# Sample-state updates of a hybrid decoder step: matmuls moved into the routing, sums kept in memory and added to the states at the end

## The chip, the cores and the metric

The kernel runs on one core of one Trainium2 chip. The metric is the device time of one execution, in microseconds (us). A core has five engines that run side by side and meet in semaphores: PE (TensorE, matmuls), DVE (VectorE), ACT (ScalarE), POOL (GpSimd) and SP (SyncE, which here only issues transfers). 16 DMA engines move data between memory and the on-chip SBUF; matmuls write to eight PSUM banks of 128 x 512 floats.

## The reference

One inference step of a one-layer decoder trunk, for 512 prompt tokens and 8 sample sequences of 4 tokens (T = 544 rows of width 1024). A token mixer is followed by a mixture of 16 experts:

```
proj = x @ w_in                                   # q, f, v, g and three conv parts
S_new = exp(b_last) * S + einsum('bhsk,bhkv->...', k * exp(b_last - b), v)   # state, per head
o     = rms(q-part of the state and of the chunk) * silu(g)
x1    = layer_norm(ALPHA * x + concat[o, yc] @ w_out)
probs = softmax(x1 @ w_router + bias); best group of 4, then its best 2 experts
y     = sum_e gate_e * (silu(x1 @ w_gate[e]) * (x1 @ w_up[e])) @ w_down[e]
out   = layer_norm(ALPHA * x1 + y)
```

For the samples the old state (8 sequences x 4 heads x 128 x 128, 2 MB) is an input and the new one an output: per sequence and head, new = decay * old + k^T v over the sequence's four tokens. This sum k^T v, the sample update, is what the change is about.

## The kernel before

All matmuls that matter for accuracy split each float32 operand into a rounded high part and a low part and run three products (ACT makes the high part, DVE the low one by a subtraction of two SBUF operands). The work runs in stages, each engine with its own program order:

- **Input projection and recurrence** (to about 266 us). POOL forms exponents (`exponents`, L575), DVE decays q and k (`decayed`, L1017), PE the pairs.
- **Output projection** (266 to 322 us and on). PE runs `mix(half, conv, tt)` (L1627): 12 matmuls for each of five token tiles, for two halves of the columns and two halves of the rows of w_out. DVE adds each tile to the residual (`add_mix`, L1152) and normalises. Behind `mix(0, False, tt)`, tt below 4, PE makes head tt's sample updates (`sample_updates`, L1639): two fp32 matmuls of 32 rows, 128 keys by 512 value columns, four sequences each. So that a matmul forms the sums of single sequences, POOL first copies the head's values into `v_msk`, once per sequence and zero elsewhere (`mask_values`, L613). There is one `v_msk` buffer, so head h waits for head h-1's matmuls. DVE forms the new states from banks 1 and 2 and the old states `s0` (`new_states`, L1164), eight operations a head. When all are made, SP stores `s0` (L480), loads ln2's parameters (L482), waits for the store (L510) and only then loads the first expert weights, since `raw[3]` and `raw[4]` lie where `s0` lay.
- **Router and routing** (322 to 375 us). PE transposes x1 and makes the logits (`turn_x1`, `logits`). DVE then runs one chain of some 60 small operations (L1211 to L1286): softmax, group and expert choice, rank (after PE's matmuls L1719, L1721), slots, and the table of token ids (after PE's L1731). In its waits PE runs `keep_clock(n)`, idle matmuls without a reader: 16 before the rank, 12 before the slots and 28 behind them. POOL gathers the rows of the first two experts' tokens from memory (`gather`, L625); PE transposes them (`x_turn`), ACT and DVE split them.
- **Experts** (375 to 666 us). Sixteen steps in a fixed order, each with six weight chunks of 1 MB, loaded by SP into a ring of eight raw buffers, split by ACT (`mhi`) and DVE (`mlo`), and used by PE. POOL stores each expert's rows to memory and gathers the next expert's tokens. `xg` holds two blocks of gathered rows.
- **End** (666 to 705 us). POOL waits for the last row store and gathers each token's two expert rows; PE weighs and sums them with diagonal matrices (`weigh`, L1837), DVE, ACT and POOL normalise, SP stores (L556, L558).

There is a branch for tokens beyond an expert's first 128; here no step of it runs, and nothing of it shows in the trace.

Of the kernel before, what the change touches and what calls it, by code (L numbers as in the profile page):

```python
# [42 lines left out]
H = 4  # L43
# [72 lines left out]
def build(nc, a):  # L116
# [5 lines left out]
    with ctx:  # L122

        x1_dram = nc.dram_tensor("x1_by_token", (T, D), F32, kind="Internal").ap()
        yg_dram = nc.dram_tensor("y_by_slot", (NBLK * P, D), F32, kind="Internal").ap()
# [29 lines left out]
        raw += [fa(68 * K, 2048), fa(68 * K + 2 * H * T, 2048)]  # L155
        s0 = fa(32 * K, 4096).rearrange("p (b h v) -> p b h v", b=DB, h=H)
        A0 = 48 * K
        xn = fa(A0, NTT * D).rearrange("p (t n) -> p t n", t=NTT)
# [23 lines left out]
        k_tok_s = fa(Q0 + H * T, 512).rearrange("p (h k) -> p h k", h=H)  # L182
        v_msk = fa(Q0 + H * T + 512, DB * P).rearrange("p (b v) -> p b v", b=DB)
        h_gain = fa(Q0 + H * T + 1536, 512)
# [21 lines left out]
        wr = fa(Z0, KT * E).rearrange("p (k e) -> p k e", k=KT)  # L206
        silu_g, hbuf = fa(64 * K, 512), fa(66 * K, 512)
        ysb = [fa(U0, D), fa(U0 + D, D)]
        diag = fa(Z0, (1 + 2 * NTT) * P).rearrange("p (i r) -> p i r", i=1 + 2 * NTT)
# [26 lines left out]
        s_su, s_st, s_o, s_oc = sem("state_update"), sem("state_ready"), sem("o_made"), sem("o_copied")  # L236
        s_vm, s_sus, s_s0n, s_sto = sem("v_masked"), sem("sample_update"), sem("sample_state"), sem("sample_states_stored")
        s_stp = sem("prompt_state_stored")
        s_selt, s_sel = sem("groups_transposed"), sem("groups_t_ready")
# [70 lines left out]
        def x_place(m):  # L310

            n = P if m % NTT < 4 else NS
            c0 = P if m == 2 * NTT - 1 else 0
            return bank[x_bank(m)][:, c0:c0 + 4 * n]

        def sum_banks(tt):
# [108 lines left out]
        def _(sp):  # L425
# [52 lines left out]
            sp.dma_start(rt[:, 448:464], a["router_bias"].unsqueeze(0).broadcast_to([P, E])).then_inc(s_wr, 16)  # L478
            sp.wait_ge(s_s0n, 2 * H)
            sp.dma_start(a["out_hgrn_sample"][0].rearrange("b h k v -> k b h v"), s0).then_inc(s_sto, 16)  # L480
            for i, name in ((2, "ln2_g"), (3, "ln2_b")):
                sp.dma_start(ln[:, i, :], a[name].broadcast_to([P, D])).then_inc(s_lnp2, 16)  # L482

# [25 lines left out]

            sp.wait_ge(s_sto, 16)  # L510
            load(3, source(5, 0, None))
# [10 lines left out]
            for tt in range(NTT):  # L522
                sp.wait_ge(s_x1, tt + 1)
                rows = P if tt < 4 else NS
                sp.dma_start(x1_dram[tt * P:tt * P + rows, :], xr[0:rows, tt, :]).then_inc(s_x1s, 16)
            load(6, source(2, 1, 0))
            moe_loads(1, 1, (4, 5))
            moe_loads(2, 2, (0,))
# [7 lines left out]
            moe_loads(E, E, (2, 3))  # L536

            sp.wait_ge(s_slot, 3)
            n_over = sp.value_load(itab[0:1, 0:1], min_val=0, max_val=NOV)
            with sp.If(0 < n_over):  # L540
                with sp.Fori(0, NOV // RING) as i:
                    for r in range(RING):
                        v = RING * i + r
                        with sp.If(v < n_over):
                            e = sp.value_load(itab[0:1, bass.ds(v + 1, 1)], min_val=0, max_val=E - 1)
                            for o, j in enumerate(OV_ORDER):
                                sp.wait_ge(m_lo, 6 * E + 6 * v + o + 1 - NRAW)
                                load(6 * E + 6 * r + o, source(j, e, e))

            for tt in range(NTT):  # L550
# [15 lines left out]
        def _(pool):  # L566
# [46 lines left out]
            def mask_values(h):  # L613
                nc.gpsimd.tensor_tensor(v_msk[0:NS], v_tok[0:NS, 4, h * P:(h + 1) * P].unsqueeze(1).broadcast_to([NS, DB, P]),
                                        seq_mask, ALU.mult).then_inc(s_vm, 1)
# [4 lines left out]
            nc.gpsimd.memset(xr[:, 4, :], 0.0).then_inc(s_xr0, 1)  # L620
            for h in range(1, H):
                pool.wait_ge(s_sus, 2 * h)
                mask_values(h)
# [8 lines left out]
            pool.wait_ge(s_x1s, 16 * NTT)  # L632
            pool.wait_ge(s_ids, 1)
            gather(0, 0)
            gather(1, 1)
            pool.wait_ge(m_t, 1)
# [23 lines left out]
            n_over = pool.value_load(itab[0:1, 0:1], min_val=0, max_val=NOV)  # L660
            with pool.If(0 < n_over):  # L661
                for v in range(NOV):
# [19 lines left out]
        def _(act):  # L682
# [158 lines left out]

            for n, j in enumerate((0, 1, 4)):
                act.wait_ge(m_raw[n], 16)
                nc.scalar.activation(split[split_slot(0, j)][0], raw[n], ACT.Copy).then_inc(m_hi, 1)


# [20 lines left out]
            def silu(bi):  # L867
                act.wait_ge(m_use, gate_count(bi))
                if not (isinstance(bi, int) and bi == 0):
                    act.wait_ge(m_h, bi)  # L870
                nc.scalar.activation(silu_g, bank[2][:, :], ACT.Silu).then_inc(m_sg, 1)
# [76 lines left out]
        def _(dve):  # L948
# [214 lines left out]

            def new_states(h):  # L1164

                for g in range(2):
                    dve.wait_ge(s_sus, 2 * h + g + 1)
                    for i in range(4):
                        bi = 4 * g + i
                        last = stt(s0[:, bi, h, :], s0[:, bi, h, :], s0_decay[:, bi * H + h:bi * H + h + 1],  # L1170
                                   bank[1 + g][:, i * P:(i + 1) * P], ALU.mult, ALU.add)
                    last.then_inc(s_s0n, 1)

            dve.wait_ge(s_o, NTT)
# [203 lines left out]
            with dve.If(0 < n_over):  # L1378
                with dve.Fori(0, NOV // RING) as i:
                    for r in range(RING):  # L1380
                        v, par = RING * i + r, r % 2
                        with dve.If(v < n_over):
# [12 lines left out]
                            dve.wait_ge(m_st[par], 16 * (E // 2 + r // 2) + 8 * RING * i)  # L1395
                            nc.vector.tensor_copy(ysb[par][:, 512:D], bank[6][:, :]).then_inc(m_yd, 1)

            ts_(diag[:, 0, :], ident, ALPHA, None, ALU.mult).then_inc(s_diag, 1)
            for tt in range(NTT):
                rows = P if tt < 4 else NS  # L1400
                for n in range(2):
                    ts_(diag[0:rows, 1 + 2 * tt + n, 0:rows], ident[0:rows, 0:rows],
                        gw[0:rows, n * NTT + tt:n * NTT + tt + 1], None, ALU.mult).then_inc(s_diag, 1)
            dve.wait_ge(s_lnp2, 32)

# [23 lines left out]
        def _(pe):  # L1429
# [264 lines left out]
            for n in range(6):  # L1694
                last_mix(n)
            pe.wait_ge(s_s0n, 2 * H)
            pe.wait_ge(s_wc, NTT)
# [12 lines left out]

            def keep_clock(n):

                idle = RA[:, 32 * K + KT * T:32 * K + KT * T + 640]
                for _ in range(n):
                    mm(bank[0][:, :], idle[:, 512:640], idle[:, 0:512], start=True, stop=True)

            keep_clock(16)
            pe.wait_ge(s_oh, 1)
# [5 lines left out]

            keep_clock(12)
            for n in range(2):
# [74 lines left out]

            keep_clock(28)
            x_turn(0, 0)
# [80 lines left out]
```

## Time and profile before

| | us |
|---|---|
| median of 3 runs | 703.26 (702.64 to 706.01) |
| the profiled execution: its own time | 706.77 |
| its span, first to last instruction | 704.9 |
| PE, DVE, ACT, POOL busy | 671.2, 503.6, 344.3, 134.9 |
| mean granted TensorE clock | 0.974 of full speed |
| moved by DMA | 162.56 MB |

The profile is of one execution. A row of a timeline has the start in us from the span's begin, the duration in us, engine, line, operation, tiles out<-in, shapes and how many instructions are merged (x12), and in brackets how long the engine had been idle and who released it. One fp32 matmul stands as two records. The granted clock is 1.00 for 2.4 GHz and 0.50 for 1.2 GHz.

### The profile page before, as it was taken

What the parts mean: (1) busy time and instruction counts of PE and PEld (TensorE: products, weight loads), DVE (VectorE), ACT (ScalarE), POOL (GpSimd) and SP (SyncE); (2) the same over time, 40 slices, a digit from 0 to 9 for tenths busy, and PEclk for the clock granted to TensorE, in tenths of its full rate; (3) what the DMA queues carried; (4) which work ended last, traced back from release to release, by engine and by line L of the source; (5) the groups of instructions that cost most, each with busy time, mean ns of one, the idle gap of its engine ahead of it and who ended that gap; (6) DMA issues with size and microseconds to landing.
All of it is one profiled execution on the core that took longest, in us unless ns stands there. A gap on an engine that the chain in (4) does not pass through costs nothing. (4 is left out here: it accounts for less than half of the span.)

```text
span 704.9 us, 9687 instructions
## 1 busy us (share of the span) xinstructions
PE 671.2 (95%) x3863; PEld 563.5 (80%) x3863; DVE 503.6 (71%) x576; ACT 344.3 (49%) x338; POOL 134.9 (19%) x81
## 2 busy tenths in 40 slices
PE   6999999988999999999978999999999999999796
PEld 5999899988997887567856888888888888888531
DVE  4326346799666284757495999999999999999526
ACT  4438412222236231011415777777777777777302
POOL 0000414433031210400021011111111111100064
PEclk9999999999999999999799999999999999999997
DMA  9951111211613005069227999999999999993163
GB/s 288 382 185 61 60 60 61 70 53 58 202 43 109 23 16 191 0 209 419 97 84 304 364 377 416 410 402 419 413 402 415 404 410 410 411 405 148 60 248 133
DMA packets 48689, 162.56 MB, mean 231 GB/s; under 512 B 4294, under 2 KB 23450, under 8 KB 36364
## 3 DMA queue, kind: packets, MB, share of 16 engines
q1 hardware_dynamic: 41756, 136.62, 51.0%
q0 software_dynamic: 6896, 25.43, 9.2%
q8 instruction: 25, 0.41, 0.2%
q14 instruction: 12, 0.10, 0.0%
HBM read 142.61 MB, written 19.44 MB: 230 GB/s over the span
## 5 line engine op out<-in xcount | busy, mean ns | idle before, releaser
L1309 DVE TENSOR_TENSOR RA<-FA,RA 128x2048 fp32r<-128x2048 f32 x93 | 212.8, 2289 | 28.6 <-ACT RA L854 28.0
L854 ACT ACTIVATE RA<-FA 128x2048 fp32r<-128x2048 f32 x93 | 178.9, 1924 | 45.0 <-PE bank L1753 28.9
L1753 PE MATMUL bank<-RA 128*128 128x512 f32 x768 | 186.1, 398 | 2.3 <-DVE RA L1314 2.1
L1753 PEld LDWEIGHTS bank<-RA 128*128 128x128 f32 x768 | 142.3, 190 | 34.0 <-DVE RA L1314 3.0
L1491 PE MATMUL bank<-RA 128*128 128x272 f32 x432 | 110.4, 292 | 0.0
L1492 PE MATMUL bank<-RA 128*128 128x272 f32 x432 | 109.7, 290 | 0.0
L1765 PE MATMUL bank<-RA 128*128 128x512 f32 x384 | 89.9, 390 | 1.4 <-DVE RA L1319 1.4
L1765 PEld LDWEIGHTS bank<-RA 128*128 128x128 f32 x384 | 72.0, 188 | 16.5 <-DVE RA L1319 1.6
L1491 PEld LDWEIGHTS bank<-RA 128*128 128x128 f32 x432 | 82.6, 191 | 0.0
L1492 PEld LDWEIGHTS bank<-RA 128*128 128x128 f32 x432 | 82.4, 191 | 0.0
L978 DVE TENSOR_TENSOR RA<-FA,RA 128x2048 fp32r<-128x2048 f32 (+1 forms) x18 | 48.6, 2700 | 28.6 <-ACT RA L712 28.3
L712 ACT ACTIVATE RA<-FA 128x2048 fp32r<-128x2048 f32 (+1 forms) x18 | 33.6, 1866 | 59.9 <-PE bank L1635 30.9
L1484 PE MATMUL bank<-RA 128*128 128x256 f32 (+1 forms) x480 | 58.8, 282 | 2.0 <-ACT FA L724 2.0
L1484 PEld LDWEIGHTS bank<-RA 128*128 128x128 f32 (+1 forms) x480 | 56.2, 172 | 4.6 <-ACT FA L724 2.4
L1635 PE MATMUL bank<-RA 128*128 128x512 f32 (+1 forms) x240 | 59.4, 405 | 0.0
L628 POOL DMA_INDIRECT FA<-x_by_token,ids x16 | 39.8, 2485 | 83.5 <-DVE ids L1286 65.1
L1635 PEld LDWEIGHTS bank<-RA 128*128 128x128 f32 (+1 forms) x240 | 41.7, 177 | 17.0 <-issue 3.2
L645 POOL DMA_DIRECT2D y_by_slot<-FA x16 | 9.1, 571 | 236.6 <-DVE FA L1326 236.6
L583 POOL TENSOR_TENSOR FA<-FA 128x1024 f32<-128x1024 f32 (+1 forms) x7 | 16.6, 2368 | 112.9 <-PE bank L1526 67.8
L759 ACT ACTIVATE FA<-FA 128x2048 f32<-128x2048 f32 (+1 forms) x7 | 13.6, 1946 | 49.6 <-POOL FA L584 49.6
L1037 DVE COPY_PREDICATED FA<-masks,bank 128x512 f32<-128x512 uint8 x28 | 20.1, 734 | 22.2 <-PE bank L1526 21.7
L1526 PE MATMUL bank<-FA 128*128 128x128 f32 x256 | 30.9, 278 | 3.9 <-DVE FA L1037 3.9
(227 smaller groups left out, 764.9 us busy)
## 6 DMA issues: line engine op xcount, KB each, us to landing
FA<-w_up SPq DMA_DIRECT2D x32, 1024.0 KB, 7.3
FA<-w_gate SPq DMA_DIRECT2D x32, 1024.0 KB, 6.9
FA<-w_down SPq DMA_DIRECT2D x32, 1024.0 KB, 7.7
FA<-w_in SPq DMA_DIRECT2D x13, 1024.0 KB, 5.0
y_by_slot<-FA POOLq DMA_DIRECT2D x16, 512.0 KB, 7.7
y_by_slot<-FA POOLq DMA_DIRECT2D x1, 4096.0 KB, 17.1
FA<-w_out SPq DMA_DIRECT2D x4, 1024.0 KB, 5.1
FA<-x_prompt SPq DMA_DIRECT2D x8, 256.0 KB, 5.8
```

Source lines behind the costliest of these rows:

```text
L628: pool.indirect_dma_start(out=xg[par], out_offset=None, in_=x1_dram, in_offset=bass.IndirectOffsetOnAxis(ap=ids[:, bi:bi + 1].bitcast(U32) ...
L712: nc.scalar.activation(split[o % 2][0][:, cs], raw[o % 3][:, cs], ACT.Copy).then_inc(s_hi, 1)
L854: nc.scalar.activation(split[split_slot(bi, j)][0], raw[place], ACT.Copy).then_inc(m_hi, 1)
L978: tt_(split[o % 2][1][:, cs], raw[o % 3][:, cs], f(split[o % 2][0][:, cs]), ALU.subtract).then_inc(s_lo, 1)
L1309: tt_(sl[1], raw[place], f(sl[0]), ALU.subtract).then_inc(m_lo, 1)
L1484: last = mm(pb[0:rows, 0:CW], xT[x_][:, kt, tok(j)], w_[:, kt, :], start=(kt == 0 and i == 0), stop=(kt == KT - 1 and i == 2))
L1491: mm(pb[:, 0:HT], lhs, xT[x_][:, kt, 0:HT], start=first, stop=end)
L1492: last = mm(ps[:, 0:HT], lhs, xT[x_][:, kt, HT:T], start=first, stop=end)
L1526: last = mm(bank[4 + p % 3][:, cols], lf[:, h, cols], rf[:, h, cols], start=True, stop=True)
L1635: last = mm(w_bank(half, tt)[0:rows, :], xT[x_][:, k0 + kt, tok(tt)], w_[:, kt, :], start=(conv and kt == 0 and i == 0), stop=(not conv an ...
L1753: last = mm(out[:, :], xgT[par][x_][:, kt, :], w[w_][:, t, :], start=(kt == 0 and i == 0), stop=(kt == KT - 1 and i == 2))
L1765: last = mm(bank[5 + g][:, :], hT[x_][:, kt, :], w[w_][:, t, 512 * g:512 * g + 512], start=(kt == 0 and i == 0), stop=(kt == 3 and i == 2))
```

## The change

The sample updates leave the output projection. PE makes heads 0 and 1 behind the logits in place of 12 of the 16 idle matmuls, head 2 behind the rank in place of 12, and head 3 behind the slots with 16 idle ones instead of 28. ACT copies each of the eight results from its bank into SBUF (`su_out`), between the first expert's weight copies. SP stores each head's 512 KB to memory (`su_dram`) ahead of the loads of expert 1's up weights; ln2's parameters are loaded behind the last expert's weights. POOL has two buffers for the masked values, and its second gather waits until all four stores have landed (its target shares space with `su_out[3]`). SP no longer stores states or waits ahead of the first expert loads. When the last weights are split, SP loads the old states again (2 MB) and the four updates (4 x 512 KB); DVE adds them with 32 operations behind the gate diagonals, and SP stores the new states ahead of the outputs.

```diff
@@ memory and SBUF
+        su_dram = nc.dram_tensor("sample_updates", (H, P, DB * P), F32, kind="Internal").ap()
+        s0_end = fa(48 * K, 4096).rearrange("p (b h v) -> p b h v", b=DB, h=H)
-        v_msk = fa(Q0 + H * T + 512, DB * P).rearrange("p (b v) -> p b v", b=DB)
+        v_msk = [fa(off, DB * P).rearrange("p (b v) -> p b v", b=DB)
+                 for off in (Q0 + H * T + 512, AT0 + NTT * D - 2 * H * T)]
+        su_out = [fa(off, DB * P) for off in (U0, U0 + DB * P, 64 * K, 60 * K)]
+        su_end = [fa(off, DB * P).rearrange("p (b v) -> p b v", b=DB) for off in (Q0, Q0 + DB * P, B0, B0 + DB * P)]
+        def update_bank(n):
+            return bank[(0, 1, 2, 3, 7, 0, 1, 2)[n]]
@@ SP
-            sp.wait_ge(s_s0n, 2 * H)
-            sp.dma_start(a["out_hgrn_sample"][0].rearrange("b h k v -> k b h v"), s0).then_inc(s_sto, 16)
-            for i, name in ((2, "ln2_g"), (3, "ln2_b")):
-                sp.dma_start(ln[:, i, :], a[name].broadcast_to([P, D])).then_inc(s_lnp2, 16)
...
-            sp.wait_ge(s_sto, 16)
             load(3, source(5, 0, None))
...
             load(6, source(2, 1, 0))
+            for h in range(H):
+                sp.wait_ge(s_sue, 2 * h + 2)
+                sp.dma_start(su_dram[h], su_out[h]).then_inc(s_sud, 16)
             moe_loads(1, 1, (4, 5))
...
             moe_loads(E, E, (2, 3))
+            sp.wait_ge(s_sud, 16 * H)
+            for i, name in ((2, "ln2_g"), (3, "ln2_b")):
+                sp.dma_start(ln[:, i, :], a[name].broadcast_to([P, D])).then_inc(s_lnp2, 16)
+            sp.wait_ge(m_lo, 6 * E - 2)
+            sp.wait_ge(m_t, E)
+            states_again()
+            sp.wait_ge(m_lo, 6 * E - 1)
+            updates_again(0)
+            updates_again(1)
+            sp.wait_ge(m_lo, 6 * E)
+            updates_again(2)
+            updates_again(3)
...
+            sp.wait_ge(s_s0n, H)
+            sp.dma_start(a["out_hgrn_sample"][0].rearrange("b h k v -> k b h v"), s0_end).then_inc(s_sto, 16)
             for tt in range(NTT):
@@ POOL
             mask_values(0)
             pool.wait_ge(s_stp, 16)
             pool.wait_ge(s_o, NTT)
             nc.gpsimd.memset(xr[:, 4, :], 0.0).then_inc(s_xr0, 1)
-            for h in range(1, H):
-                pool.wait_ge(s_sus, 2 * h)
+            mask_values(1)
+            for h in range(2, H):
+                pool.wait_ge(s_sus, 2 * (h - 1))
                 mask_values(h)
...
             pool.wait_ge(s_ids, 1)
+            pool.wait_ge(s_vm, H)
             gather(0, 0)
+            pool.wait_ge(s_sud, 16 * H)
             gather(1, 1)
@@ ACT
-            for n, j in enumerate((0, 1, 4)):
+            def copy_update(n):
+                act.wait_ge(s_sus, n + 1)
+                nc.scalar.activation(su_out[n // 2][:, 512 * (n % 2):512 * (n % 2) + 512], update_bank(n)[:, :],
+                                     ACT.Copy).then_inc(s_sue, 1)
+
+            def first_hi(n, j):
                 act.wait_ge(m_raw[n], 16)
                 nc.scalar.activation(split[split_slot(0, j)][0], raw[n], ACT.Copy).then_inc(m_hi, 1)
+            for n in range(4):
+                copy_update(n)
+            first_hi(0, 0)
+            first_hi(1, 1)
+            for n in range(4, 2 * H):
+                copy_update(n)
+            first_hi(2, 4)
@@ DVE
-            def new_states(h):
...
-                if tt < H:
-                    new_states(tt)
...
+            dve.wait_ge(s_end, 16 * (H + 1))
+            for h in range(H):
+                for bi in range(DB):
+                    last = stt(s0_end[:, bi, h, :], s0_end[:, bi, h, :], s0_decay[:, bi * H + h:bi * H + h + 1],
+                               su_end[h][:, bi, :], ALU.mult, ALU.add)
+                last.then_inc(s_s0n, 1)
             dve.wait_ge(s_lnp2, 32)
@@ PE
                 for g in range(2):
-                    if h:
-                        pe.wait_ge(s_s0n, 2 * h + g - 1)
-                    mm(bank[1 + g][:, :], k_tok_s[0:NS, h, :], v_msk[0:NS, 4 * g:4 * g + 4, :],
+                    n = 2 * h + g
+                    if n >= 5:
+                        pe.wait_ge(s_sue, n - 4)
+                    mm(update_bank(n)[:, :], k_tok_s[0:NS, h, :], v_msk[h % 2][0:NS, 4 * g:4 * g + 4, :],
                        start=True, stop=True).then_inc(s_sus, 1)
...
                 mix(0, False, tt)
-                if tt < H:
-                    sample_updates(tt)
...
-            keep_clock(16)
+            sample_updates(0)
+            sample_updates(1)
+            keep_clock(4, bank[5])
             pe.wait_ge(s_oh, 1)
...
-            keep_clock(12)
+            sample_updates(2)
...
-            keep_clock(28)
+            sample_updates(3)
+            pe.wait_ge(s_sue, 4)
+            keep_clock(16, bank[3])
             x_turn(0, 0)
```

## Rows read from the trace of the kernel before

**Rows 1.** The page's first part: busy us, share of the span, instructions

```profile
PE 671.2 (95%) x3863; PEld 563.5 (80%) x3863; DVE 503.6 (71%) x576; ACT 344.3 (49%) x338; POOL 134.9 (19%) x81
```

**Rows 2.** Timeline of PE, 290 to 297 us: head 2's sample updates

```profile
294.37 1.98 PE L1645 MATMUL bank<-FA 32*128 32x512 f32 x4 [0.54 <-POOL FA L614]
296.28 1.24 PE L1635 MATMUL bank<-RA 128*128 128x512 f32 x3
```

**Rows 3.** Timeline of PE, 346 to 385 us: routing and first expert

```profile
348.26 5.39 PE L1715 MATMUL bank<-RA 128*128 128x512 f32 x16
355.15 0.22 PE L1719 MATMUL bank<-FA 128*128 128x96 bf16 x1 [1.50 <-DVE FA L1247]
...
360.66 0.50 PE L1731 MATMUL bank<-FA 128*128 128x24 bf16 x10 [2.32 <-DVE FA L1283]
...
371.26 1.23 PE L1743 MATMUL bank<-FA 128*128 128x128 f32 x8 [1.05 <-DMA FA<-x_by_token,ids]
374.63 7.35 PE L1753 MATMUL bank<-RA 128*128 128x512 f32 x24 [2.14 <-DVE RA L1314]
381.82 1.12 PE L1743 MATMUL bank<-FA 128*128 128x128 f32 x8
```

**Rows 4.** Busy time by stretch: PE, PEld, DVE, ACT, POOL, clock, DMA, GB/s

```profile
348.00:351.00 3.00, 3.00 (x14) 2.39 (x13) 2.09 (x12) 1.76 (x2) 0.00 (x0) 0.50 0.00 0
```

**Rows 5.** Timeline of DVE, 341 to 375 us: ends of the routing chain

```profile
348.37 0.23 DVE L1211 TENSOR_TENSOR FA<-bank,FA 128x64 f32<-128x64 f32 x1 [7.00 <-PE bank L1670]
...
362.51 6.69 DVE L1301 TENSOR_TENSOR RA<-FA,RA 128x2048 fp32r<-128x2048 f32 x3
...
373.29 1.29 DVE L1314 TENSOR_TENSOR RA<-bank,RA 128x512 fp32r<-128x512 f32 x2
```

**Rows 6.** Timeline of ACT, 280 to 388 us: the first three weight copies

```profile
349.42 5.50 ACT L844 ACTIVATE RA<-FA 128x2048 fp32r<-128x2048 f32 x3
```

**Rows 7.** Timeline of POOL: an exponent subtraction and head 1's mask

```profile
105.41 3.94 POOL L584 TENSOR_TENSOR FA<-FA 128x1024 f32<-128x1024 f32 x1
...
286.00 1.89 POOL L614 TENSOR_TENSOR FA<-FA 32x1024 f32<-32x1024 f32 x1 [18.96 <-PE bank L1645]
```

**Rows 8.** Timeline of DVE: beside those, and the other steps used

```profile
107.52 2.98 DVE L1024 TENSOR_TENSOR FA<-FA 128x1088 f32<-128x1088 f32 x1
110.42 1.28 DVE L1025 TENSOR_TENSOR FA<-FA 128x1088 f32<-128x1088 f32 x1
...
268.10 0.69 DVE L1136 TENSOR_TENSOR FA<-FA 128x512 f32<-128x512 f32 x1
...
285.38 2.14 DVE L1170 SCALAR_TENSOR_TENSOR FA<-FA,bank 128x128 f32<-128x128 f32 x8
```

**Rows 9.** Transfers by line: KB each, median us from issue to landing

```profile
y_by_slot<-FA POOLq DMA_DIRECT2D x16, 512.0 KB, 7.7
...
out_hgrn_sample<-FA SPq DMA_DIRECT2D x1, 2048.0 KB, 9.3
...
FA<-x_by_token,ids POOLq DMA_INDIRECT x16, 10.9
FA<-y_by_slot,slot_i POOLq DMA_INDIRECT x10, 6.3
...
FA<-state_hgrn SPq DMA_DIRECT2D x1, 0.5 KB, 12.2
```

**Rows 10.** The chain that ended last: start us, us, what

```profile
673.82 0.98 POOL FA L671
...
675.10 6.20 DMA FA<-y_by_slot,slot_i
...
681.34 16.72 PE bank L1841 x36
```

**Rows 11.** Timeline of DVE, 655 to 685 us: last weight split, end

```profile
659.64 2.28 DVE L1309 TENSOR_TENSOR RA<-FA,RA 128x2048 fp32r<-128x2048 f32 x1
...
681.19 1.30 DVE L1412 BATCH_NORM_STATS2 FA<-bank 128x6 f32<-128x512 f32 x2 [11.98 <-PE bank L1841]
```

More of the change, by code:

```diff
@@ L237, in build @@
         s_vm, s_sus, s_s0n, s_sto = sem("v_masked"), sem("sample_update"), sem("sample_state"), sem("sample_states_stored")
+        s_sue, s_sud, s_end, s_ovd = (sem("sample_update_copied"), sem("sample_update_stored"), sem("states_and_updates_in"),
+                                      sem("overflow_done"))
         s_stp = sem("prompt_state_stored")
@@ L536, in _, with states_again, updates_again @@
             moe_loads(E, E, (2, 3))
+            def states_again():
+                sp.dma_start(s0_end, a["state_hgrn"][0].rearrange("b h k v -> k b h v")).then_inc(s_end, 16)
+            def updates_again(h):
+                sp.dma_start(su_end[h].rearrange("p b v -> p (b v)"), su_dram[h]).then_inc(s_end, 16)
+            sp.wait_ge(s_sud, 16 * H)
[10 more added lines that the diff above has]
+            updates_again(3)
             sp.wait_ge(s_slot, 3)
@@ L540, in _ @@
             with sp.If(0 < n_over):
+                sp.wait_ge(s_end, 16 * (H + 1))
                 with sp.Fori(0, NOV // RING) as i:
@@ L548, in _ @@
                                 load(6 * E + 6 * r + o, source(j, e, e))
+                sp.wait_ge(s_ovd, 1)
+                states_again()
+                for h in range(H):
+                    updates_again(h)
+            sp.wait_ge(s_s0n, H)
+            sp.dma_start(a["out_hgrn_sample"][0].rearrange("b h k v -> k b h v"), s0_end).then_inc(s_sto, 16)
             for tt in range(NTT):
@@ L613, in mask_values @@
             def mask_values(h):
-                nc.gpsimd.tensor_tensor(v_msk[0:NS], v_tok[0:NS, 4, h * P:(h + 1) * P].unsqueeze(1).broadcast_to([NS, DB, P]),
+                nc.gpsimd.tensor_tensor(v_msk[h % 2][0:NS], v_tok[0:NS, 4, h * P:(h + 1) * P].unsqueeze(1).broadcast_to([NS, DB, P]),
                                         seq_mask, ALU.mult).then_inc(s_vm, 1)
@@ L661, in _ @@
             with pool.If(0 < n_over):
+                pool.wait_ge(s_end, 16 * (H + 1))
                 for v in range(NOV):
@@ L868, in silu @@
                 act.wait_ge(m_use, gate_count(bi))
-                if not (isinstance(bi, int) and bi == 0):
+                if isinstance(bi, int) and bi == 0:
+                    act.wait_ge(s_sud, 16 * H)
+                else:
                     act.wait_ge(m_h, bi)
@@ L1162, in add_mix @@
                 chain[0] += 1
-            def new_states(h):
[L1166 to L1172, printed above, removed]
             dve.wait_ge(s_o, NTT)
@@ L1396, in _ @@
                             nc.vector.tensor_copy(ysb[par][:, 512:D], bank[6][:, :]).then_inc(m_yd, 1)
+                nc.vector.memset(rt[:, 441:442], 0.0).then_inc(s_ovd, 1)
+                dve.wait_ge(s_end, 32 * (H + 1))
             ts_(diag[:, 0, :], ident, ALPHA, None, ALU.mult).then_inc(s_diag, 1)
@@ L1403, in _ @@
                         gw[0:rows, n * NTT + tt:n * NTT + tt + 1], None, ALU.mult).then_inc(s_diag, 1)
+            dve.wait_ge(s_end, 16 * (H + 1))
+            for h in range(H):
+                for bi in range(DB):
+                    last = stt(s0_end[:, bi, h, :], s0_end[:, bi, h, :], s0_decay[:, bi * H + h:bi * H + h + 1],
+                               su_end[h][:, bi, :], ALU.mult, ALU.add)
+                last.then_inc(s_s0n, 1)
             dve.wait_ge(s_lnp2, 32)
@@ L1695, in _ @@
                 last_mix(n)
-            pe.wait_ge(s_s0n, 2 * H)
             pe.wait_ge(s_wc, NTT)
@@ L1709, in _, with keep_clock @@
             logits(NTT - 1).then_inc(s_lg, 1)
-            def keep_clock(n):
+            def keep_clock(n, to):
                 idle = RA[:, 32 * K + KT * T:32 * K + KT * T + 640]
                 for _ in range(n):
-                    mm(bank[0][:, :], idle[:, 512:640], idle[:, 0:512], start=True, stop=True)
-            keep_clock(16)
+                    mm(to[:, :], idle[:, 512:640], idle[:, 0:512], start=True, stop=True)
+            sample_updates(0)
+            sample_updates(1)
+            keep_clock(4, bank[5])
             pe.wait_ge(s_oh, 1)
@@ L1800, in step @@
                 gate_up(bank[3], par, split_slot(bi, 5), 1, count_of(bi, 5))
-            keep_clock(28)
+            sample_updates(3)
+            pe.wait_ge(s_sue, 4)
+            keep_clock(16, bank[3])
+            pe.wait_ge(s_sue, 2 * H)
             x_turn(0, 0)
```

## The prediction

> **What bounds the kernel now.** The page comes first: PE is busy for 95% of the span [rows 1], so each stage is asked whether PE waits there. In the output projection (266 to 348 us) it is the bound: its timeline has no gap but one of 0.54 us, ahead of head 2's state updates [rows 2]. One head's updates (four records: two fp32 matmuls of two passes) hold PE from 294.37 to 296.28, 1.91 us [rows 2], and there are four heads. In the routing (348 to 375 us) it is not: DVE starts at 348.37 when the logits end and runs one serial chain to 362.5 [rows 5]; PE fills its waits with idle matmuls and still sits idle 1.50, 2.32 and 1.05 us, then 2.14 us for DVE's low half of the gathered x [rows 3]. At the end the chain is the row gather that lands at 681.3 and then 16.7 us of PE [rows 10].
>
> **The change, part by part.**
> 1. *Updates out of the projection.* PE loses 4 x 1.91 = 7.6 us and the 0.54 us stall, 8.2 us. DVE loses four groups of eight state operations at 2.14 us [rows 8], which lay in its waits: nothing. Late next would be the second half's low weights, but they hang on the end of the first half's last matmul, which moves along. So the logits end 8.2 us sooner: **-8.2**. Bounds: -7.6 (the stall reappears) to -8.2.
>
> 2. *The second mask moves.* POOL forms head 1's masked values now right behind its memset at about 267.1 us, 1.89 us long [rows 7], two SBUF inputs. Does that touch DVE? At 105.41 a POOL tensor_tensor ran to 109.35 [rows 7]; DVE's multiply, started at 107.52, took 2.98 us, while the same kind took 1.28 right behind [rows 8]. It ended 1.2 us after POOL did: it had waited for all of it. DVE operations with one input in PSUM are not held: eight of them took their usual 2.14 us beside the mask of 286.00 [rows 7, 8]. At 268.10 DVE scales head outputs, two SBUF inputs, 0.69 us [rows 8]; it would be held to 269.0, and the transposition on PE that waits for it comes with it: **+0.85** (0 to 1.2, if PE cannot hide it).
>
> 3. *Updates 0 and 1 in the wait for the choice.* The 16 idle matmuls took 5.39 us at a clock that began at half (0.50 [rows 4], the 1.2 GHz level, after the 16-column logits). Eight update records cost about 3.2 us at the half clock (3.3 of them) and 4.7 x 0.48 = 2.2 us at full, and four idle ones at most 1.0 (half an update record each or less): 6.4 us, against the 6.9 from 348.26 to 355.15 [rows 3]. Nothing on PE itself; 0 to +2.5 if the clock stayed low (twice 3.8 and twice 0.9 make 9.4 us).
>
> 4. *Masks 2 and 3 in the routing.* This is the term that I count highest. They are released when updates 0 and 1 are done (about 352 and 354 us in the old times), and run 1.89 us each while DVE is in its chain of small operations, most of which read two SBUF operands, each waiting for the one before. By rows 7 and 8 the first such operation waits for the end of the mask. A reduction or two with one input may pass, so 1.7 us each: **+3.4**. PE then idles some 4 us ahead of the rank matmuls, and the clock falls: **+0.2** for six short matmuls. Bounds 0 (no hold on such small operations) and 2 x 1.89 + 0.3 = +4.1.
>
> 5. *ACT.* Eight copies of a bank join, about 0.6 us each by estimate (512 columns, where a weight copy of 2048 takes 5.50/3 = 1.8 us [rows 6]). Six and two of the three weight copies fit into ACT's old gap. The third weight copy stands behind copies 6 and 7, and these behind head 3's update, which is issued behind the slot matmuls. In old times: these end at about 362.3, just ahead of DVE's 362.51 [rows 5]; update to 364.2 at full clock or 366.1 at half; copy 7 to 364.8 or 366.7; the weight copy 1.8 us more, so 366.6 or 368.5. DVE wants it 2 x 2.2 us after 362.51, at 366.9 [rows 5]. Late by 0 or 1.6 us; DVE's next steps run without a gap to 373.29 [rows 5] and release PE at 374.63 [rows 3]. **+0.9**, bounds 0 and 1.9.
>
> 6. *Stores of the updates and the second gather.* Four stores of 512 KB pass through SP ahead of expert 1's up weights, which are needed a step later: nothing. POOL's second gather now waits for the last store. That is issued about 367 (old times) and lands in 3 to 7.7 us (the store of a y block [rows 9]); a gather takes 10.9 [rows 9]: 381 to 386. PE wants it at 381.82 [rows 3], which steps 4 and 5 move by 4.5 to 386.3. I take 0, bounds 0 and +3. The first six expert loads start up to 40 us sooner, behind nothing that they can delay: 0.
>
> 7. *The tail.* The update reads follow the last weight split, which ends at 661.9 [rows 11]; with 7.7 us they are in by 669.6. The 2 MB of old states, 12.2 us [rows 9], are asked for some 9 us earlier. The last y store shares their last microsecond: **+0.4** (0 to 1.5). DVE then has 32 state operations, at 2.14/8 us each 8.6 us, and 11.98 us of idle time ahead of 681.19 to put them in [rows 8, 11]: begun by 669.6 they end by 678.2. Nothing, with 3 us in hand. They now read two SBUF operands, so each row gather on POOL waits for the one under way: **+0.4**. The store of the new states, 2 MB in 9.3 us when little else ran [rows 9], starts at about 678, among the gathers that feed PE (6.3 us each [rows 9]). The gather issued at 675.10 (tile 1's first) lands at 681.3, and the next follow at 1.28 us [rows 10], so tile 2's land at about 683.9 and 685.1; PE, at 16.72/9 = 1.86 us for each, takes them at 685.1 and 686.9: 1 to 2 us in hand. A gather in the expert loop takes 10.9 us beside weight loads instead of 6.3, so sharing is felt. I take **+1.0**, from 0 up to the case in which the two queues share the DMA engines evenly: what lands at 683.9 then lands 6 us after that, and PE is 5 to 5.7 us late.
>
> Here a page matters. The Trainium skill, "DMA: Bandwidth & Descriptors", section "Queues, rings and completion order", says that a DMA engine takes turns between queues by whole packets of typically 9 to 17 descriptors. By that a turn of the 512-byte rows of the state store would be as long as a turn of the gather or longer, and the tail would cost 5.7 instead of 1.0. No row of the kernel before shows a store of short rows beside a gather; I read it as one row per turn, which favours the gather's 4 KB rows.
>
> **Sum.** -8.2 + 0.85 + 3.6 + 0.9 + 0.4 + 0.4 + 1.0 = -1.05 us. The profiled execution took 706.8 us (span 704.9), the median of the runs is 703.26; taken off the median that is **702.2 us**. A measurement of this kernel can tell about 0.5%, 3.5 us, from no change.
>
> **The rivals.**
> - *The masks hold DVE little* (chance 0.22). The routing's operations take 0.15 to 0.3 us, and no row shows POOL beside such short ones. Against it: nothing in rows 7 and 8 depends on length. Terms 2 and 4 fall away: -1.05 - 4.45 = -5.5 us, 697.8.
> - *The state store starves the last gathers* (0.13, with the masks holding DVE). Place: the gathers of tiles 2 and 3, from 678 us. Price 5.7 in place of 1.0: +3.65 us, 706.9. It makes the change slower than before as soon as it costs over 2 us. For it: the 10.9 us of the expert loop. Against: PE, not the gathers, sets the pace from 681.3 on [rows 10].
> - *The second gather comes late* (0.07). If the last update store and the gather, with the weight loads behind them, take 2 us more each than their rows 9, the gather lands at 390 against 386.3: +3.7 to the sum, +2.65, 705.9.
> - *The change doesn't do what it says* (0.05). If the projection were held by something else that ended at the same time, the updates would leave 2 us of gain only: +5, 708.4. PE's gapless timeline speaks against it.
> - *As forecast* (0.53): 702.2, own range 699.5 to 705.
>
> **How the numbers follow.** Within 0.5% is 699.7 to 706.8. Of the forecast's 0.53 I put 0.06 below, 0.44 within, 0.03 above. The first rival gives 0.18 below and 0.04 within; the two late-gather rivals, whose centres lie near the upper edge, 0.09 within and 0.11 above; the fifth case 0.05 above. So faster 0.24, the same 0.57, slower 0.19. The range reaches from the first rival's centre to a little past the starved tail: 697.7 to 708.0.
>
> **What would show it.** The projection ends and the logits end some 7.3 us sooner (341, not 348.3). In the routing, two DVE operations with two SBUF inputs last about 1.9 us instead of 0.24, each ending with a POOL mask, and the first expert's first matmul stands at 374.6 - 7.3 + 4.5 = 371.8 us. The third weight split of expert 0 waits for ACT by 0 to 1.6 us. PE's second transposition waits for no DMA. In the tail DVE's 32 operations end by 678, and PE waits under 1.5 us more for gathers than now. I am wrong if DVE's chain of 14 us keeps its length (then the first rival), or if PE has gaps between tiles at the end (then the second), or if the logits end at 343 or later.

## The result, and the profile after

The changed kernel takes 711.94 us (median of 4 executions, 709.45 to 712.88) against 704.63 (702.64 to 706.71) for the kernel before in the same sitting: ratio 1.0108, 95% interval 1.0078 to 1.0138. It is 7.3 us slower, where 1 us faster was forecast, and lies outside the forecast range.

The profiled execution of after is the fastest of its four (709.45, span 707.6), that of before one of its slower ones (706.77, span 704.9). So the two traces differ by only 2.7 us. They show where time came and went; how much it is in all, the medians say.

| stretch, us | before | after | difference | forecast |
|---|---|---|---|---|
| mixing stage, from its 272.6 / 272.2 to its end | 49.6 | 39.0 | -10.6 | -8.2 |
| logits' end to expert 0's first matmul | 26.4 | 31.2 | +4.8 | +4.5 |
| expert 0's first matmul to the last y store's issue | 292.2 | 292.2 | 0.0 | 0 |
| last y store's issue to the end | 38.1 | 48.8 | +10.7 | +1.8 |

In these two traces the last y store is issued 8.0 us sooner, at 658.82 instead of 666.80, and the end gave back 10.7. The 8.0 hold 2.2 us that the table does not show: 0.4 ahead of the mixing stage, and 1.8 between its end and the logits' end. That last part is 26.0 us long in before and 24.3 in after, and 23.8 to 26.2 in the eleven other traces of the changed kernel and its variants, by where in it the granted clock falls to 0.50; its 1.8 us are chance. So is the 0.0 in the third row: in the repeat of the change that stretch takes 294.6 us.

The first part of the page of after, and then the busy time by stretch, of before and of after (columns as in [rows 4]):

```profile
PE 665.0 (94%) x3827; PEld 555.9 (79%) x3827; DVE 507.5 (72%) x576; ACT 349.7 (49%) x346; POOL 138.0 (20%) x81
```

```profile
296.20:300.80 4.60, 4.60 (x13) 3.35 (x12) 1.82 (x8) 0.00 (x0) 1.89 (x1) 0.63 0.01 4
```

```profile
296.20:300.80 4.60, 4.60 (x22) 3.71 (x21) 2.29 (x1) 0.50 (x1) 0.00 (x0) 1.00 0.23 28
...
336.00:339.00 3.00, 3.00 (x4) 1.00 (x3) 2.35 (x14) 0.87 (x2) 0.00 (x0) 0.50 0.00 0
354.00:357.00 3.00, 3.00 (x5) 0.89 (x4) 3.00 (x2) 1.14 (x3) 2.15 (x1) 0.50 0.04 10
360.00:363.00 3.00, 2.78 (x17) 2.28 (x15) 2.69 (x11) 0.18 (x1) 0.95 (x1) 1.00 0.97 373
666.00:668.00 2.00, 2.00 (x6) 0.71 (x4) 2.00 (x9) 0.00 (x0) 2.00 (x1) 1.00 0.00 0
...
680.00:682.00 2.00, 2.00 (x4) 0.97 (x3) 0.00 (x0) 0.00 (x0) 1.60 (x2) 0.50 1.04 410
```

PE's busy share fell from 95% [rows 1] to 94%: work left PE, but idle time came. Before, the matmuls behind head 2's updates ran at a mean granted clock of 0.63 (13 in 4.6 us); after, 22 stand in the same window at 1.00. In the routing the clock is 0.50 from the logits to behind 357 us, updates and all. From 666 to 668, where the row gathers should go out, DVE and POOL are both busy all the time and no DMA engine moves a byte.

The routing, PE's timeline of after (answers to [rows 3]):

```profile
335.46 7.19 PE L1694 MATMUL bank<-FA 32*128 32x512 f32 x8
342.58 2.08 PE L1761 MATMUL bank<-RA 128*128 128x512 f32 x4
345.22 0.26 PE L1767 MATMUL bank<-FA 128*128 128x96 bf16 x1 [0.56 <-DVE FA L1287]
...
352.67 3.76 PE L1694 MATMUL bank<-FA 32*128 32x512 f32 x4
356.35 5.48 PE L1761 MATMUL bank<-RA 128*128 128x512 f32 x16
361.67 1.12 PE L1791 MATMUL bank<-FA 128*128 128x128 f32 x8
366.62 7.28 PE L1801 MATMUL bank<-RA 128*128 128x512 f32 x24 [3.84 <-DVE RA L1354]
373.74 1.12 PE L1791 MATMUL bank<-FA 128*128 128x128 f32 x8
```

The timelines of DVE and of POOL, after, in the same stretch (answer to [rows 5, 7]):

```profile
339.23 0.24 DVE L1269 TENSOR_TENSOR FA<-FA 128x80 f32<-128x80 f32 x1
339.50 1.82 DVE L1270 TENSOR_TENSOR FA<-FA 128x80 f32<-128x80 f32 x1
...
343.01 0.24 DVE L1271 TENSOR_REDUCE FA<-FA 128x5 f32<-128x80 f32 x1
343.28 1.55 DVE L1272 TENSOR_TENSOR FA<-FA 128x80 f32<-128x80 f32 x1
...
358.89 2.29 DVE L1341 TENSOR_TENSOR RA<-FA,RA 128x2048 fp32r<-128x2048 f32 x1 [1.45 <-ACT RA L886]
```

```profile
339.32 1.90 POOL L647 TENSOR_TENSOR FA<-FA 32x1024 f32<-32x1024 f32 x1 [71.45 <-PE bank L1694]
342.74 1.99 POOL L647 TENSOR_TENSOR FA<-FA 32x1024 f32<-32x1024 f32 x1 [1.51 <-PE bank L1694]
```

Two operations of 0.24 us last 1.82 and 1.55, and each ends some 0.1 us behind a mask (341.22, 344.73): +2.9 us. A reduction with one input, at 343.01, runs beside the second mask in its usual 0.24. The first four updates (eight records) take 7.19 us and the four idle matmuls 2.08, 9.3 together. The third weight split waits 1.45 us for ACT. Nothing stands ahead of PE's second transposition at 373.74: the second gather is in time.

The end of after: DVE's and POOL's timelines, the queue of SP, and PE.

```profile
662.62 8.49 DVE L1449 SCALAR_TENSOR_TENSOR FA<-FA 128x128 f32<-128x128 f32 x32 [1.40 <-DMA FA<-sample_updates]
```

```profile
658.82 0.53 POOL L681 DMA_DIRECT2D y_by_slot<-FA  x1 [9.36 <-DVE FA L1366]
665.61 6.36 POOL L708 DMA_INDIRECT FA<-y_by_slot,slot_i  x1 [6.26 <-issue]
672.28 0.98 POOL L708 DMA_INDIRECT FA<-y_by_slot,slot_i  x1 [0.31 <-issue]
```

```profile
659.43 8.83 PE L1892 MATMUL bank<-FA 128*128 128x512 f32 x16 [1.88 <-DVE FA L1440]
678.99 21.72 PE L1892 MATMUL bank<-FA 128*128 128x512 f32 x44 [10.73 <-DMA FA<-y_by_slot,slot_i]
```

The transfers of after (answers to [rows 9]):

```profile
sample_updates<-FA SPq DMA_DIRECT2D x4, 512.0 KB, 2.6
FA<-sample_updates SPq DMA_DIRECT2D x4, 512.0 KB, 7.8
out_hgrn_sample<-FA SPq DMA_DIRECT2D x1, 2048.0 KB, 21.4
...
FA<-y_by_slot,slot_i POOLq DMA_INDIRECT x10, 10.2
```

The chain of after (answers to [rows 10]):

```profile
665.61 13.25 DMA FA<-y_by_slot,slot_i
...
678.99 21.73 PE bank L1892 x44
```

The first row gather occupies POOL for 6.36 us instead of 0.98: it ends 0.9 us behind the last of the 32 additions (662.62 + 8.49 = 671.11). That is +5.4 us. The store of the new states starts when the additions end, together with this gather, and PE, which waits for it, starts 7.0 us after its end at 671.97. In before the first gather, issued at 672.53 and as long as the next one, 0.98 us, was over at 673.51, and PE began 3.5 us later. PE's timeline of before:

```profile
676.98 1.95 PE L1841 MATMUL bank<-FA 128*128 128x512 f32 x4 [0.74 <-DMA FA<-y_by_slot,slot_i]
```

That is +3.6 us. From there to PE's last matmul before took 21.1 us and after takes 21.7: +0.7. After its long pause PE begins at the half clock (0.50 at 680 to 682), while before it ran at 1.00 with short waits for gathers. And the first gather starts 6.8 us behind the y store's issue instead of 5.7: +1.1. Together 10.7 (rounded parts). No experiment isolates the +1.1. It is also there without the additions (6.5 us), and it is gone (5.1 to 5.3) in the three traces of the change and its variants in which the y store goes out some 1.5 us later against the reads of the updates. That fits the prediction's term for the y store sharing time with these reads, forecast at 0.4.

### The profile page after: what moved, and what is told of

The parts are those of the page before. It is cut to its first block and busy times, and to the rows that moved or that the text cites. A ratio compares the mean times of both kernels' runs of the same rounds, so it can differ in the third digit from the quotient of the medians.

```text
span 707.6 us, 9633 instructions
## 1 busy us (share of the span) xinstructions
PE 665.0 (94%) x3827; PEld 555.9 (79%) x3827; DVE 507.5 (72%) x576; ACT 349.7 (49%) x346; POOL 138.0 (20%) x81
## 5 line engine op out<-in xcount | busy, mean ns | idle before, releaser
L1683 PE MATMUL bank<-RA 128*128 128x512 f32 (+1 forms) x240 | 56.8, 395 | 0.0
L662 POOL DMA_INDIRECT FA<-x_by_token,ids x16 | 38.9, 2433 | 29.9 <-PE bank L1791 12.2
L1892 PE MATMUL bank<-FA 128*128 128x512 f32 (+1 forms) x60 | 30.5, 671 | 12.6 <-DMA FA<-y_by_slot,slot_i 10.7
```

What stands on the lines that cost most here:

```text
L662: pool.indirect_dma_start(out=xg[par], out_offset=None, in_=x1_dram, in_offset=bass.IndirectOffsetOnAxis(ap=ids[:, bi:bi + 1].bitcast(U32) ...
L1683: last = mm(w_bank(half, tt)[0:rows, :], xT[x_][:, k0 + kt, tok(tt)], w_[:, kt, :], start=(conv and kt == 0 and i == 0), stop=(not conv an ...
L1892: ins = mm(bank[i][0:rows, :], diag[0:rows, d, 0:rows], src[0:rows, tt, 512 * g:512 * g + 512], start=first, stop=last)
```

## The experiments

Each ran beside the kernel before, in one of three sittings; its medians there were 704.17, 703.63 and 704.23 us. A ratio is worked out from all executions of its own sitting, and is not quite that of the two medians.

**The end: moving the store, and taking the additions out.** First, SP waits for the last gathers before it stores the states; second, the same without the additions:

```diff
             sp.wait_ge(s_s0n, H)
+            for n in range(2):
+                sp.wait_ge(s_ga[NTT - 1][n], 16)
             sp.dma_start(a["out_hgrn_sample"]...
```

```diff
-            for h in range(H):
-                for bi in range(DB):
-                    last = stt(s0_end[:, bi, h, :], ...)
-                last.then_inc(s_s0n, 1)
+            nc.vector.memset(rt[:, 441:442], 0.0).then_inc(s_s0n, H)
```

> The change with one edit: SP issues the store of the new states only when the last two row gathers have landed. Theory A (the 32 state additions, two SBUF inputs each and back to back, hold POOL's first row gather until the last of them) expects the first gather on POOL still about 6.4 us long, but landing 3.3 us after it, as before the change, instead of 6.9: the first sum on PE 3 to 4 us sooner than in the change, time 3 to 4 us below the change. Rival B (the state store in the DMA queues is the whole loss) expects the long first gather gone too and the time 8 us or more below the change. Rival C (the loads of states and updates delay the last y store) expects no more than 1 us.

> The run e2 without the 32 state additions (they are left out; a memset gives their signal). Theory A expects POOL's first row gather back at 1.0 us and the time 5 to 6 us below e2, some 8 us below the kernel before, with the front of the change kept whole. Rival B expects no difference to e2. Rival C (transfers, not the additions) expects the gap from the last y store to the first gather's end to stay at 13 us.

Measured: 708.61 us, ratio 1.0075 (1.0042 to 1.0107), and 700.70 us, 0.9952 (0.9927 to 0.9977). The timeline of POOL with the store last, and without the additions:

```profile
667.94 6.36 POOL L710 DMA_INDIRECT FA<-y_by_slot,slot_i  x1 [6.18 <-issue]
674.61 0.98 POOL L710 DMA_INDIRECT FA<-y_by_slot,slot_i  x1 [0.30 <-issue]
```

```profile
668.04 0.98 POOL L710 DMA_INDIRECT FA<-y_by_slot,slot_i  x1 [5.93 <-issue]
669.32 0.98 POOL L710 DMA_INDIRECT FA<-y_by_slot,slot_i  x1 [0.30 <-issue]
```

With the store out of the way the gather is held as long as ever. Without the additions it is not held, and 7.9 us are gone, more than the 5 to 6 expected. Yet that kernel, whose output lacks the additions, is only 3.4 us below before, where some 8 were expected: the front is worth less by the medians than by the two traces, whose 8.0 us hold 2.2 of chance. The store's own part is the first of these against the change: PE waits 7.06 us instead of 10.73, 3.7 less in the traces; by the ratios (1.0075 against 1.0086 and 1.0108) 1 to 2 us, which the intervals can't tell from nothing.

**The additions in pieces.** They stay, and DVE waits for its own completion behind every second one (with the store last, and with the store where the change has it); then the change with one such wait behind each head's eight, three of which stand between additions:

```diff
                 for bi in range(DB):
                     last = stt(s0_end[:, bi, h, :], ...)
+                    if bi % 2 and bi < DB - 1:
+                        link(last)
                 last.then_inc(s_s0n, 1)
+                dve.wait_ge(s_s0n, h + 1)
```

```diff
                 last.then_inc(s_s0n, 1)
+                dve.wait_ge(s_s0n, h + 1)
```

> The run e2 with DVE waiting for its own completion behind every second state addition. If POOL gets the shared port only when DVE's queue runs dry for a moment (theory A1), the first gather takes 1 to 2 us and the time is 3 to 5 us below e2, though the additions take longer. If any running sequence of such additions keeps POOL out regardless of short breaks (A2), the first gather lasts until the last addition, 6.4 us or more, and the time is that of e2 or 1 to 3 us above.

> The change with the breaks between the additions, the state store left where the change has it. The run with both edits was 0.35% under the kernel before. If the hold of the first gather is the main loss and the store a smaller one, this run's gathers start in time, the state store starts at about 674 beside the fourth gather, and the last gathers are 2 to 4 us late: 702 to 705 us. If PE, not the gathers, sets the pace there (as the prediction had it), the store costs under 1 us: 700 to 702.

> The change with only three breaks in the additions: DVE waits for its own completion behind each head's eight. If POOL gets the port only where DVE's queue runs dry (A1), the first gather ends behind the first break after its start, so it lasts 1 to 3.3 us instead of 6.4, and the next gathers wait likewise, about 2.3 us apart, until the additions end at the same place as before: time 3 to 6 us below the change, above the run with 15 breaks. If the length of each single addition matters rather than the breaks, the first gather stays at 6 us.

Measured: 700.53 us, 0.9965 (0.9934 to 0.9996); 700.61, 0.9954 (0.9927 to 0.9981); 700.27, 0.9951 (0.9926 to 0.9977). The change itself in the same sitting as the second:

> The change itself, unedited, on the chip of the next three runs: 7 to 8 us above the kernel before (709 to 712 us), POOL's first row gather 6.4 us long and landing 13 us after its start, the clock of the updates in the routing at the half level as in the first profile (0.50 from 336 to 357 us).

It took 710.35 us, 1.0086 (1.0045 to 1.0127), its first gather 6.54 us. The timelines of the third kernel (a wait behind each eight), DVE's and POOL's, and its transfers:

```profile
663.43 8.87 DVE L1449 SCALAR_TENSOR_TENSOR FA<-FA 128x128 f32<-128x128 f32 x32
```

```profile
666.41 0.98 POOL L708 DMA_INDIRECT FA<-y_by_slot,slot_i  x1 [4.81 <-issue]
667.70 1.00 POOL L708 DMA_INDIRECT FA<-y_by_slot,slot_i  x1 [0.30 <-issue]
669.00 1.09 POOL L708 DMA_INDIRECT FA<-y_by_slot,slot_i  x1 [0.30 <-issue]
```

```profile
out_hgrn_sample<-FA SPq DMA_DIRECT2D x1, 2048.0 KB, 17.1
FA<-y_by_slot,slot_i POOLq DMA_INDIRECT x10, 8.1
```

Three waits that cost DVE 0.4 us (8.87 against 8.49) bring the ratio from 1.0086 to 0.9951, 9.5 us, and turn the loss into a gain of 4. They are worth as much as the removal of the additions: nothing else of the additions costs time that these runs can tell. Against the expectations, the first gained 8.1 us where 3 to 5 were expected, the third 9.5 where 3 to 6 were, and the second is where it was put if PE sets the pace (700 to 702). With the waits in, the place of the store matters no more (0.9965 and 0.9954), though the gathers' median landing is 8.1 us beside it. My expectation that a gather would wait up to the next break was wrong. The groups end at about 665.6, 667.9 and 670.1 (an estimate: four equal parts of the 8.87 us), and the gather of 666.41 began and ended within a group, at its usual length. Why eight additions in a row let it pass and 32 don't, no run here shows.

**The routing.** First the masks of heads 2 and 3 formed ahead, in two more buffers; then the same without the four idle matmuls; then the change with only the third weight copy ahead of copies 6 and 7:

```diff
-                 for off in (Q0 + H * T + 512, AT0 + NTT * D - 2 * H * T)]
+                 for off in (Q0 + H * T + 512, AT0 + NTT * D - 2 * H * T, 64 * K, 60 * K)]
...
             mask_values(1)
+            pool.wait_ge(s_on, NTT)
             for h in range(2, H):
-                pool.wait_ge(s_sus, 2 * (h - 1))
                 mask_values(h)
```

```diff
-            keep_clock(4, bank[5])
```

```diff
-            for n in range(4, 2 * H):
+            for n in range(4, 6):
                 copy_update(n)
             first_hi(2, 4)
+            for n in range(6, 2 * H):
+                copy_update(n)
```

> The change with masks 2 and 3 formed right behind the attention output's normalisation, into buffers that the update copies and a gather use only later, so that POOL is idle in the routing. The prediction's term 4 expects DVE's routing chain 2.9 us shorter (two operations of 1.82 and 1.55 us back at 0.24). But PE ran updates 0 and 1 and the four idle matmuls at the half clock until 344.66, where the choice came at 345.16: so the rank can come only 0.5 us sooner, and the gain at the first expert is about 0.5 us (PE bound) plus nothing later, unless the clock rises. Rival: it is 3 us sooner (DVE bound alone). Time against the change: -0.5 against -3 us.

> e5 without the four idle matmuls behind update 1 (2.08 us at the half clock). With early masks alone the first expert came 0.5 us sooner, because PE was the bound. If that reading is right, the rank now comes 2.6 us sooner than in the change, and so does the first expert (28.6 us behind the logits instead of 31.2). Time 2.5 us below the change. If the masks cost nothing and the idle matmuls were the only bound, the same would come from dropping them alone; but then DVE's two long operations, which end at 345.16 in the change, would not be there to be seen.

> The change with ACT's third weight copy ahead of copies 6 and 7. DVE's wait of 1.45 us ahead of the third split goes, so the first expert stands 1.4 us sooner behind the logits (29.7 us), if the second gather, whose release comes 1.9 us later at most, still lands in time. Time 1.4 us below the change. Rival: the second gather is late and takes it back.

| | us | ratio (interval) | logits' end to first expert |
|---|---|---|---|
| change (the repeat) | 710.35 | 1.0086 (1.0045 to 1.0127) | 31.2 |
| masks early | 708.29 | 1.0074 (1.0032 to 1.0115) | 30.6 |
| and no idle four | 707.03 | 1.0051 (1.0023 to 1.0078) | 28.6 |
| third copy first | 707.09 | 1.0065 (1.0037 to 1.0093) | 29.9 |

PE's timeline with the masks early, and then without the four idle ones:

```profile
334.44 7.19 PE L1694 MATMUL bank<-FA 32*128 32x512 f32 x8
341.56 2.08 PE L1761 MATMUL bank<-RA 128*128 128x512 f32 x4
343.44 0.30 PE L1767 MATMUL bank<-FA 128*128 128x96 bf16 x1
```

```profile
337.14 7.19 PE L1694 MATMUL bank<-FA 32*128 32x512 f32 x8
344.26 0.26 PE L1766 MATMUL bank<-FA 128*128 128x96 bf16 x1
```

With the masks away the rank matmul waits for nothing but PE's own queue, and only 0.5 us are won; with the idle four gone too, 2.6. So two paths lay side by side, 0.5 us apart: DVE held by the masks, and PE at the half clock. The third copy is worth 1.3 us. The stretch came out near what was expected each time. The intervals of the times are too wide to show so little, so what these three edits are worth is read from one trace each.

**Together, and with the clock tried.** All of it (waits, store last, masks early, idle four gone, third copy first), and then eight idle matmuls of 128 rows put ahead of the first update to lift the clock:

```diff
+            keep_clock(8, bank[5])
             sample_updates(0)
             sample_updates(1)
```

> Breaks and late store as in e3, and in the routing: masks 2 and 3 early, the four idle matmuls behind update 1 dropped, and ACT's third weight copy ahead of copies 6 and 7. PE then ends update 1 some 7.2 us behind the logits, as against 6.9 for DVE's choice, so the rank comes 2.4 us sooner than in the change, and the third weight split 1.4 us more: first expert 3.5 to 4 us sooner behind the logits (27.3 us instead of 31.2). The second gather moves 2 us later and may then cost up to 1 us. Time 3 to 4 us below e3: 697 us, 1% under the kernel before. If the clock on the way into the experts falls longer because PE does less, 1 to 2 us of that are lost.

> e7 with eight idle matmuls of 128 rows ahead of update 0. In all profiles so far the granted clock stayed at 0.50 through the updates (32 rows) for 15 us and more and rose only behind the 16 idle matmuls of 128 rows. If rows of the array decide, the clock rises during the eight (3.4 us), the eight update records then take 3.8 us instead of 7.2, and the rank comes at the same time as in e7, with the clock at 1.00 for at least update 0: time equal to e7 within 1 us, or lower by 1 if the experts start warmer. If the clock doesn't rise, the rank comes 3.4 us later and the time is 3 us above e7.

Measured: 697.23 us, 0.9898 (0.985 to 0.9947), the fastest that still computes everything; and 697.34, 0.9904 (0.9871 to 0.9936). The second one's timeline of PE and its busy time by stretch:

```profile
335.05 3.78 PE L1768 MATMUL bank<-RA 128*128 128x512 f32 x8
338.77 7.19 PE L1701 MATMUL bank<-FA 32*128 32x512 f32 x8
```

```profile
344.00:347.00 3.00, 3.00 (x10) 1.20 (x9) 0.19 (x1) 1.60 (x3) 0.00 (x0) 0.50 0.43 175
...
358.00:361.00 3.00, 3.00 (x10) 2.34 (x9) 2.88 (x6) 0.00 (x0) 0.00 (x0) 0.62 0.98 345
```

The clock did not rise. The rank came 3.7 us later and the first expert 3.9 us later behind the logits (30.9 against 27.1), and in the traces this is still whole at the last y store (issued at 658.02, not 654.04); the spans are 696.7 and 694.2. The medians agree, but the two intervals together leave room for 4 us, so they do not contradict the loss.

**What the updates cost before.** The kernel before, without the sample updates, masks 1 to 3 and the additions:

```diff
                 if tt < H:
-                    sample_updates(tt)
...
-                    new_states(tt)
```

> The kernel before with the sample updates, their last three masks and the state additions left out (the old states are stored as they are): the most that the projection can give. The prediction's term 1 (four times 1.91 us and one stall of 0.54) expects the stretch from the attention output to the end of the logits 8.2 us shorter and 695 to 696 us. The two profiles (11 us between the same instructions, matmuls behind an update 0.2 us per tile slower, and a clock of 0.63 in one stretch) expect 10 to 11 us and 692 to 694 us.

Measured: 694.23 us, 0.985 (0.9809 to 0.9891), 9.4 us less, between the two expectations. Its mixing stage is one gapless row, 39.0 us to the next:

```profile
272.10 39.18 PE L1632 MATMUL bank<-RA 128*128 128x512 f32 x168
311.12 1.04 PE L1679 MATMUL bank<-FA 128*128 128x128 f32 x8
```

## Why the prediction was wrong, point by point

*Step 1* was right in kind and small in size: 9.4 us by the medians, 10.6 by the profiles, forecast 8.2. Missing in the term were the matmuls behind the updates. PE's timeline of before:

```profile
290.76 3.08 PE L1635 MATMUL bank<-RA 128*128 128x512 f32 x12
...
296.28 4.62 PE L1635 MATMUL bank<-RA 128*128 128x512 f32 x12
```

Twelve matmuls take 2.8 us in the row without updates (39.0 us for 168). Behind head 2's updates, and their stall of 0.54 us, they take 4.6, at the clock of 0.63. The other groups ahead of and between the updates are slower by 0.2 to 0.3 us each, 2.5 us in all with this one, and 7.6 + 0.54 + 2.5 make the 10.6. The logits end 12.8 us sooner in the trace (335.46), not 7.3; 1.8 of the excess is the chance named above.

*Step 2*: the stall that was forecast stands ahead of the head outputs' transposition, 0.54 us for 0.85, in PE's timeline of after:

```profile
268.48 0.66 PE L1661 MATMUL bank<-FA 128*128 128x128 f32 x4 [0.54 <-DVE FA L1188]
```

*Step 3*: "nothing" was right by only 0.5 us. PE needed 9.3 us, the upper bound's 9.4, since the clock stayed low; it was hidden by DVE being held. Had step 4 not come true, step 3 would have cost about 2.4 us (an estimate: PE free at 344.66, DVE's choice then at 342.27). *Step 4*, counted highest, held: 2.9 us for 3.4, on two operations of 0.24 us, so the first rival (masks hold DVE little) is out. *Step 5*: 1.45 us, within 0 to 1.6, taken 0.9. *Step 6*: right, the second gather was in time, and with it the third rival is out. The routing as a whole came to +4.8 for +4.5.

*Step 7* failed, in the sentence "each row gather on POOL waits for the one under way: +0.4". It priced a wait for one operation. The trace shows the first gather waiting for the whole row of 32 additions, 5.4 us. Two more terms hang on it: the store and the first gather start in the same instant (+3.6), and PE begins at the half clock behind its pause of 10.73 us (+0.7). One term of 0.4 us grew to 9.7; that the breaks alone bring the time from 710.35 to 700.61 and 700.27 shows it. Nor had the prediction a rival for it: "the state store starves the last gathers" lies in the same stage, but at the gathers of tiles 2 and 3, not at the first one, and has another cause. That store, 1.0 us in the sum and 5.7 at most, cost 3.7 in the traces where it started with the first gather. Moving the store away won 1 to 2 us by the ratios and left the gather held, and with the additions broken up the store beside the gathers costs nothing that can be told. The bound that was missing needed no new row: if the hold is handed on from addition to addition, it lasts the 8.6 us of all 32 (four times 2.14), less what passed before the gather. The prediction put the additions into DVE's idle time and asked only whether DVE had room, not who shares a path with it meanwhile.

The Trainium skill, "SBUF — State Buffer", section "Who interferes with whom", says that a DVE instruction with two SBUF inputs and a GpSimd instruction that reads SBUF exclude each other, the later one blocked for the whole of the other. The masks agree (0.24 us to 1.82 and 1.55). For the gather the rule speaks of one instruction, and the trace shows it waiting for the whole row of 32; with eight at a time it waited for none that shows in its duration. There the measurement decides, and the page's rule gives neither.

With the breaks the tail, from the last y store on, is 37.6 to 40.0 us long, against 38.1 before and 39.9 forecast, and the kernel stands at 0.9954 and 0.9951 of before, 700 us on the scale of 703.26: 2.2 us below the forecast of 702.2, and step 1 was short by 1.2 to 2.4. The rival that the change doesn't do what it says is out: the mixing stage is 10.6 us shorter, not 2. That the kernel with the waits lands so near 702.2 is in part luck: step 3 was wrong on PE's time and cost nothing only because step 4's hold covered it.

## What to carry to other kernels

Filling an engine's idle time is free only if no other engine shares its path in that time: look at what POOL issues in the window, above all gathers on whose landing PE waits. A long run of DVE operations with two SBUF inputs, each queued right behind the last, should be broken by a wait; placing it behind the gathers' issue is the other way, which no run here tried. And price idle matmuls as well as real ones at the lower clock until a row shows that it rose.

## What the runs showed of the hardware

- 32 additions of 0.27 us back to back held a row gather on POOL from 0.98 to 6.36 us (6.54 in the repeat, 6.36 in the four other kernels that keep them in one row). With one wait behind every eight, the first three gathers took 0.98 to 1.09. Why is open.
- A POOL operation of 1.9 us on SBUF operands held DVE operations of 0.24 us with two SBUF inputs up to its end, to 1.82 and 1.55 us; a reduction with one input beside it kept its 0.24.
- The granted clock stood at 0.50 (the 1.2 GHz level) in the windows of 336 to 339 and 354 to 357, through 32-row updates and four idle matmuls, and also at 344 to 347 with eight 128-row idle ones (3.78 us) ahead; behind the 16 idle ones of 5.48 us it was 1.00.
- A 2 MB store of short rows landed in 8.7 us alone and in 21.4 beside the gathers it had started with, whose median went from 6.3 to 10.2. Started later, beside gathers already under way, it landed in 17.1 and theirs in 8.1, at no cost in time that can be told.
